# Side steps of a two-block layer kernel on one core: attention, gate and second output set apart, delta-rule scores on unscaled keys

## The chip, the cores and the metric

The kernel runs on one core of one Trainium2 chip. The metric is the time of one execution on the device in microseconds (us). The engines' names in the profile are PE (TensorE, matmuls and 128x128 transposes), PEld (its weight loads), DVE (VectorE), ACT (ScalarE), POOL (GpSimd) and SP (SyncE, here the queue that loads the weights).

## The reference, cut to what matters

256 tokens of width 2048, fp32 throughout. Two blocks follow each other. The first projects the normed input to an mLSTM and a gated delta rule, gates their outputs and projects them back. The second is attention over dilated windows beside a gated linear attention (GLA), then a feed-forward part of width 5632.

```python
# first block: the delta rule, 16 heads of 128, chunks of 64
qkv = _causal_conv_silu(dn_qkv, dn_conv_w)
dq = _l2norm(_heads(dq, DN_HEADS)); dk_ = _l2norm(_heads(dk_, DN_HEADS))
kk = jnp.einsum('cbhtd,cbhsd->cbhts', kc, kc)
a_mat = jnp.where(strict, bc[..., :, None] * kk * decay_mat, 0.0)
lhs = a_mat + jnp.eye(CHUNK, dtype=a_mat.dtype)
rhs = jnp.concatenate([vc * bc[..., None], kc * (bc * jnp.exp(gam))[..., None]], axis=-1)
sol = lax.linalg.triangular_solve(lhs, rhs, left_side=True, lower=True, unit_diagonal=True)
# second block: gate of the GLA, attention weights
log_a_f = jax.nn.log_sigmoid(lr_f @ gla_gate_w_fwd[l] + gla_gate_b_fwd[l]) / GLA_GATE_TAU
p = jnp.exp(logits - m); s = jnp.sum(p, axis=-1, keepdims=True)
gla_out = (_merge_heads_2(o).astype(x.dtype) * gla_norm_w[l]) * jax.nn.silu(gr)
mixed = jnp.concatenate([attn_out, gla_out], axis=-1) @ w_out[l]
```

The kernel solves the triangular system by inverting 32-wide diagonal blocks and joining them to blocks of 64 and 128 (the last level covers a whole tile of 128 tokens, so the chunk of 64 need not be kept).

## The kernel before, in words

All large products are fp32 products made of three reduced ones: weight_hi with x_hi, weight_lo with x_hi, weight_hi with x_lo. ACT makes weight_hi as a rounded copy of the raw weights, DVE makes weight_lo as the difference. The products are cut into 780 half slots (`HALVES`, `NH`). On PE a half slot is its side steps and then one product of 12 matmuls of 128x512 (`product`, lines L1323 to L1325). In a half slot s ACT and DVE do their side steps too, and `split(s + 3)`: ACT the weight_hi copy of 128x1024 (L1351), which waits for product s − 1, DVE the weight_lo difference (L1749). SP loads a chunk of 1 MB raw weights for two half slots at a time, five half slots or so ahead of use.

Everything else is a side step. `side_table()` puts each step's name at a half slot with `put(slot, step, ...)`, mostly counted from `END[job]`, the half slot behind a job's last product; each engine runs its part of the steps in the order of this one table, ahead of that slot's product or split. POOL and SP run theirs in the table's order alone. A step waits on semaphores for the parts of other engines that it needs (`at("dve:alog", half, c)`). Buffers of 128x1024 (blocks of the `arena`) and four side banks of PSUM are given out by `block_table` and `bank_table`, from the steps' lifetimes.

The steps that the change touches:

- Delta rule, four groups g of four heads. From s = `END[dz{g}]` + 1: `dk` (eight transposes of k on PE, squares with accumulation on ACT, a Square of q's 128x1024), `dss` (sums of q's squares by 16 matmuls with a column of ones, L961; then a power on POOL and the factors on DVE), `dkscale` (DVE scales k by the factor ck, which is the inverse norm times beta), `dkc` (eight transposes back, evicted to block kt), `drhs`, `ddecay`, `dmask` (decays and masks), `dsc` (scores of k with kt and of q), `nout`/`nin` (32-wide blocks to DRAM and back, one per partition), `dinv` (their inverses, some 65 operations on POOL, end L2335), `tout`/`tin` (back), `dT` (transposed), `dX`/`dY` for widths 64 and 128 (`LEVELS`; joins), `dv`, `du0`, `dbu`, `du1`, `do` (values, solution, output), `donorm`, `dgate`, `dout`.
- mLSTM, in the same stretch: `msq` (norm of the output; POOL's power of 128x4), `mgated` (DVE's four products), `mout` (PE's transposes).
- Gate of the GLA: `ggate2` (ACT: Abs, Exp, Ln of 128x1024 one behind the other, L1614 to L1616), `ggate3` (DVE).
- Attention: two halves, four pairs c of heads each. `alog` (PE's scores of 128x256, L1261; DVE adds the bias and takes the maximum, L2172; ACT's exponentials with sums, L1663), `anorm` (DVE reciprocal L2177, POOL multiply of 128x1024, L2279), `aturn` (eight transposes, L888), `apv`.
- Second output, in the second block: `ggated` (DVE's four products of 128x256, L1755), `gout` (eight transposes), twice, for hp 0 and 1.

L888, L1351, L1749, L1752, L1755 and L2279 are lines of helpers (transpose, copy, tensor_tensor, tensor_scalar, scalar_tensor_tensor, POOL's tensor_tensor).

## Time and profile before

| | |
|---|---|
| median of 3 runs | 2401.85 us (2401.59 to 2402.27) |
| the profiled execution, its own time | 2399.88 us |
| its span | 2398.2 us |
| granted clock of PE, mean | 0.997 |
| busy PE, DVE, ACT, POOL | 99%, 59%, 50%, 10% |
| product matmuls on PE (three lines, two kinds of input) | 9312 |
| weights from DRAM | 423.59 MB read, 179 GB/s over the span |

The own time of the profiled execution is its span and what lies around it. Matmul rows show length from a modelled end, so neighbours overlap; the distance between two starts is what one costs. A row with "x4" holds four instructions. The granted clock is in parts of full speed, 2.4 GHz; 0.50 is 1.2 GHz.

### The profile page before, as it was taken

What the parts mean: (1) busy time and instruction counts of PE and PEld (TensorE: products, weight loads), DVE (VectorE), ACT (ScalarE), POOL (GpSimd) and SP (SyncE); (2) the same over time, 40 slices, a digit from 0 to 9 for tenths busy, and PEclk for the clock granted to TensorE, in tenths of its full rate; (3) what the DMA queues carried; (4) which work ended last, traced back from release to release, by engine and by line L of the source; (5) the groups of instructions that cost most, each with busy time, mean ns of one, the idle gap of its engine ahead of it and who ended that gap; (6) DMA issues with size and microseconds to landing.
All of it is one profiled execution on the core that took longest, in us unless ns stands there. A gap on an engine that the chain in (4) does not pass through costs nothing.

```text
span 2398.2 us, 28559 instructions
## 1 busy us (share of the span) xinstructions
PE 2374.9 (99%) x11522; PEld 1948.8 (81%) x11522; DVE 1426.6 (59%) x1689; ACT 1189.5 (50%) x1653; POOL 233.3 (10%) x332
## 2 busy tenths in 40 slices
PE   9999999999999999999999999999999999999998
PEld 7888888888888888888887778678888888888886
DVE  6655665565566545665865555566554555556775
ACT  6544453454445345555646445466444444446664
POOL 0052004205200430000000010100000000000000
PEclk9999999999999999999999999999999999999999
DMA  6555455455545554765674444456655665555554
GB/s 209 194 171 163 143 191 171 149 172 171 163 141 192 170 165 161 237 202 196 213 232 157 151 157 139 141 176 221 194 186 188 193 193 185 189 188 193 193 194 140
DMA packets 235969, 430.72 MB, mean 180 GB/s; under 512 B 27492, under 2 KB 30445, under 8 KB 235838
## 3 DMA queue, kind: packets, MB, share of 16 engines
q1 hardware_dynamic: 222848, 413.30, 52.5%
q10 hardware_dynamic: 12990, 15.60, 2.2%
q8 instruction: 91, 1.49, 0.2%
q14 instruction: 40, 0.33, 0.0%
HBM read 423.59 MB, written 5.28 MB: 179 GB/s over the span
## 4 chain that ended last, share of the span: by engine, by line
PE 95%; DVE 2%; ACT 2%; issue 1%; POOL 0%; ACTq 0%; POOLq 0%; DVEq 0%
PE gemm L1323 29%; PE gemm L1325 28%; PE gemm L1324 28%; PE side L888 3%; DVE weight_lo L1749 1%; PE side L993 1%; PE side L1246 1%; ACT weight_hi L1351 1%; ACT arena L1663 0%; DVE arena L1749 0%; PE side L1285 0%; PE side L898 0%; DVE stats L2172 0%; PE side L1059 0%; PE side L997 0%
## 5 line engine op out<-in xcount | busy, mean ns | idle before, releaser
L1749 DVE TENSOR_TENSOR weight_lo<-weight_raw,weight_hi 128x1024 fp32r<-128x1024 f32 x780 | 971.0, 1248 | 775.6 <-ACT weight_hi L1351 775.2
L1351 ACT ACTIVATE weight_hi<-weight_raw 128x1024 fp32r<-128x1024 f32 x780 | 821.7, 1056 | 825.0 <-PE gemm L1325 806.8
L1323 PE MATMUL gemm<-weight_hi,x_hi 128*128 128x512 f32 x2368 | 943.8, 399 | 3.4 <-DVE x_lo L1755 2.1
L1325 PE MATMUL gemm<-weight_hi,x_lo 128*128 128x512 f32 x2368 | 924.3, 390 | 0.0
L1324 PE MATMUL gemm<-weight_lo,x_hi 128*128 128x512 f32 x2368 | 923.3, 390 | 0.0
L1323 PEld LDWEIGHTS gemm<-weight_hi,x_hi 128*128 128x128 f32 x2368 | 445.8, 188 | 103.2 <-issue 12.0
L1325 PEld LDWEIGHTS gemm<-weight_hi,x_lo 128*128 128x128 f32 x2368 | 445.2, 188 | 94.9
L1324 PEld LDWEIGHTS gemm<-weight_lo,x_hi 128*128 128x128 f32 x2368 | 446.0, 188 | 89.4 <-issue 1.4
L1323 PE MATMUL gemm<-weight_hi,lhs_hi 128*128 128x512 f32 x736 | 287.1, 390 | 0.0
L1325 PE MATMUL gemm<-weight_hi,lhs_lo 128*128 128x512 f32 x736 | 286.4, 389 | 0.0
L1324 PE MATMUL gemm<-weight_lo,lhs_hi 128*128 128x512 f32 x736 | 286.4, 389 | 0.0
L2279 POOL TENSOR_TENSOR stats<-stats,minus_half 128x4 f32<-128x4 f32 (+4 forms) x20 | 28.1, 1407 | 1886.8 <-DVE stats L1752 1886.6
L1325 PEld LDWEIGHTS gemm<-weight_hi,lhs_lo 128*128 128x128 f32 x736 | 138.2, 188 | 28.7
L1324 PEld LDWEIGHTS gemm<-weight_lo,lhs_hi 128*128 128x128 f32 x736 | 138.2, 188 | 28.5
L1323 PEld LDWEIGHTS gemm<-weight_hi,lhs_hi 128*128 128x128 f32 x736 | 138.2, 188 | 28.4
L1749 DVE TENSOR_TENSOR lhs_lo<-arena,lhs_hi 128x512 fp32r<-128x512 f32 x184 | 125.9, 684 | 0.5 <-ACT lhs_hi L1351 0.5
L2279 POOL TENSOR_TENSOR arena<-arena 128x60 f32<-128x60 f32 (+25 forms) x252 | 120.2, 477 | 33.0 <-DMA arena<-delta_blocks 13.6
L1351 ACT ACTIVATE arena<-side 128x512 f32<-128x512 f32 (+2 forms) x101 | 53.8, 570 | 132.3 <-PE side L888 57.7
L1351 ACT ACTIVATE lhs_hi<-arena 128x512 fp32r<-128x512 f32 x184 | 113.4, 616 | 1.1 <-PE gemm L1325 1.1
L888 PE MATMUL side<-constants,arena 128*128 128x128 f32 (+3 forms) x662 | 89.1, 276 | 9.4 <-POOL arena L2279 7.7
L888 PEld LDWEIGHTS side<-constants,arena 128*128 128x128 f32 (+3 forms) x662 | 77.1, 142 | 22.8 <-POOL arena L2279 9.3
L1420 ACT ACTIVATE arena<-gemm,stats 128x512 f32<-128x512 f32 x66 | 41.8, 686 | 44.7 <-PE gemm L1325 44.7
(189 smaller groups left out, 1035.6 us busy)
## 6 DMA issues: line engine op xcount, KB each, us to landing
weight_raw<-in_w_in_dram SPq DMA_DIRECT2D x207, 1024.0 KB, 5.1
weight_raw<-in_w_out_dram SPq DMA_DIRECT2D x48, 1024.0 KB, 5.0
weight_raw<-in_w_gate_dram SPq DMA_DIRECT2D x44, 1024.0 KB, 5.1
weight_raw<-in_w_up_dram SPq DMA_DIRECT2D x44, 1024.0 KB, 5.1
weight_raw<-in_w_down_dram SPq DMA_DIRECT2D x44, 1024.0 KB, 5.0
arena<-rel_line ACTq DMA_DIRECT2D x8, 384.0 KB, 5.3
arena<-in_x_dram SPq DMA_DIRECT2D x4, 512.0 KB, 9.7
arena<-delta_blocks ACTq DMA_DIRECT2D x16, 128.0 KB, 5.1
```

The source lines that it names most:

```text
L888: return e.transpose(o, i, IDN[0:n, 0:n])
L993: m = e.matmul(p[:, (h % 2) * T:(h % 2 + 1) * T], yk[:, h * T:h * T + P], y[:, h * T:(h + 1) * T], start=True, stop=True)
L1246: m = e.matmul(o, *both[x][z], start=z == 0, stop=z == len(both[x]) - 1)
L1323: e.matmul(pair[i][:, :], xh[:, s], wh, start=first, stop=False)
L1324: e.matmul(pair[i][:, :], xh[:, s], wl, start=False, stop=False)
L1325: m = e.matmul(pair[i][:, :], xl[:, s], wh, start=False, stop=last)
L1351: return e.activation(o, i, ACT.Copy, scale=scale)
L1420: s = e.activation(part(b, i), pair_of(key)[i][:, :], ACT.Tanh, scale=hr[:, i:i + 1])
L1749: return e.tensor_tensor(o, x, y, op)
L2279: return e.tensor_tensor(o, x, y, op)
```

## The change

The delta rule: q and k are each transposed seven half slots behind the end of their job (`dnorm`), ACT squares them in PSUM with accumulation, and the ones-matmuls, the scaled copy of k, its transposes and block kt are gone. The scores are between unscaled k. The factor ck is put on where results are evicted: for the 32-wide blocks it goes to DRAM (`cout`, 1024 elements of 4 bytes, written with a non-contiguous side) and back with one value per row (`nout`), and POOL multiplies the blocks of 128x1024 by it at the head of `dinv`; for `dX` the copy on ACT becomes a multiply on DVE; for `dbu` the subtraction becomes four operations that multiply by −ck and add. Everything from `dT` on comes one half slot later.

The gate: ACT's three functions become three steps (`ggabs`, `ggexp`, `ggln`), each direction's in other half slots, with Exp of both directions in one and Ln of both in one.

Attention: the exponentials become a step `aexp` two half slots behind `alog`; `anorm` is one half slot earlier and stands ahead of the next `alog`. Transposes stay.

Second output: `ggated` and `gout` of hp = 1 come one half slot later.

```diff
-        put(s, "dk", g, 0), put(s, "dk", g, 1)
-        put(s + 1, "dss", g)
-        put(s + 2, "dkscale", g)
-        put(s + 4, "dkc", g, 0), put(s + 4, "dkc", g, 1)
+        for key in (f"dk{g}", f"dq{g}"):
+            put(END[key] + 7, "dnorm", key, 0), put(END[key] + 7, "dnorm", key, 1)
+        put(s + 1, "dss", g), put(s + 3, "cout", g)
...
-        put(s + 30, "dT", g, 0), put(s + 30, "dT", g, 1)
+        put(s + 31, "dT", g, 0), put(s + 31, "dT", g, 1)
...
-        put(s + 46, "dout", g, 0), put(s + 46, "dout", g, 1)
+        put(s + 47, "dout", g, 0), put(s + 47, "dout", g, 1)
...
-        put(s + 4 + 4 * d, "ggate2", d), put(s + 7 + 4 * d, "ggate3", d)
+        put(s + 4 + d, "ggate2", d), put(s + 6 + d, "ggabs", d)
+        put(s + 8, "ggexp", d), put(s + 10, "ggln", d), put(s + 12 + d, "ggate3", d)
...
-            put(s + 4 + 2 * c, "alog", half, c), put(s + 7 + 2 * c, "anorm", half, c)
+            put(s + 4 + 2 * c, "alog", half, c), put(s + 6 + 2 * c, "aexp", half, c)
+            put(s + 6 + 2 * c, "anorm", half, c)
             put(s + 9 + 2 * c, "aturn", half, c)
...
-    put(t + 1, "ggated", hp), put(t + 2, "gout", hp, 0), put(t + 2, "gout", hp, 2)
+    put(t + 1 + hp, "ggated", hp), put(t + 2 + hp, "gout", hp, 0), put(t + 2 + hp, "gout", hp, 2)
...
+        def cout(g):
+            w.wait_ge(*at("dve:dss:ck", g))
+            e.dma_start(c_dram[g].rearrange("n p -> p n"), stat(NT * HB, "ck", g),
+                        allow_slow_non_contiguous=True).then_inc(sem("dma:cout"), 16)
...
+            src = bass.AP(tensor=c_dram.tensor, offset=g * NT * HB * P, ap=[[0, NSUB], [SUB, P // NSUB], [1, SUB]])
+            w.wait_ge(*at("dma:cout", g))
+            e.dma_start(blk("S", g)[:, 3 * SUB * SUB // 4:3 * SUB * SUB // 4 + SUB], src).then_inc(sem("dma:cin"), 16)
...
-        def dss(g):
-            w.wait_ge(*at("act:dk", g, 0))
-            p, sq = open_bank("dss", g), blk("sq", g)
-            for i in range(NT):
-                for h in range(HB):
-                    m = e.matmul(p[:, i * HB + h:i * HB + h + 1], sq[:, h * T + i * P:h * T + (i + 1) * P], ONE[:, 0:1],
-                                 start=True, stop=True)
-            m.then_inc(sem("pe:dss"))
...
-            y = blk("kt", g) if q in (0, 1, 4) else blk("y", f"dq{g}")
+            y = yk if q in (0, 1, 4) else blk("y", f"dq{g}")
...
-            if i == 0:
-                sq = claim("sq", g)
-                w.wait_ge(*at("dve:convsilu", f"dq{g}"))
-                e.activation(sq, blk("y", f"dq{g}"), ACT.Square)
...
+        def dnorm(key, i):
+            g, p = number_of(key), bank("dnorm", key, i)
+            z = i * HB + (NT * HB if kind_of(key) == "dk" else 0)
+            w.wait_ge(*at("pe:dnorm", key, i))
             for h in range(HB):
+                s = e.activation(p[:, h * P:(h + 1) * P], p[:, h * P:(h + 1) * P], ACT.Square,
+                                 accum_out=stat(4 * HB, "squares", g)[:, z + h:z + h + 1])
...
+        def dX(g, wd):
+            X, p, hw, ck = blk("X", g), bank("dX", g, wd), wd // 2, stat(NT * HB, "ck", g)
+            w.wait_ge(*at("pool:dinv:zero", g))
+            w.wait_ge(*at("dve:dss:ck", g))
+            w.wait_ge(*at("pe:dX", g, wd))
+            rows, cols = (slice(0, P), slice(0, T)) if wd < P else (slice(hw, P), slice(X6, BLK))
+            tt(X[rows, cols].rearrange("p (n x) -> p n x", x=hw), p[rows, 0:2 * HB * hw].rearrange("p (n x) -> p n x", x=hw),
+               over(ck[rows, :], 2, hw), ALU.mult).then_inc(sem("dve:dX"))
...
-            tt(b, b, bank("dbu", g), ALU.subtract).then_inc(sem("dve:dbu"))
+            w.wait_ge(*at("dve:dss:ck", g))
+            p, nck = bank("dbu", g), stat(NT * HB, "nck", g)
+            for h in range(HB):
+                sl = slice(h * P, (h + 1) * P)
+                s = stt(b[:, sl], p[:, sl], nck[:, HB + h:HB + h + 1], b[:, sl], ALU.mult, ALU.add)
...
             w.wait_ge(*at("dma:unit", g))
+            w.wait_ge(*at("dma:cin", g))
+            after(tt(N, N, over(blk("S", g)[:, 3 * SUB * SUB // 4:3 * SUB * SUB // 4 + SUB], 1, SUB), ALU.mult))
```

In the order of PE's instructions, before, at the half slot behind the gate sums (`fsum` is L932 to L935; gemm_0 and gemm_1 are the products' PSUM tiles):

```order
L1323 MATMUL gemm_1<-weight_hi,x_hi 128x512
L1324 MATMUL gemm_1<-weight_lo,x_hi 128x512
L1325 MATMUL gemm_1<-weight_hi,x_lo 128x512
L932 MATMUL side<-gate_work,constants 128x8
L933 MATMUL side<-gate_work,constants 128x8
L934 MATMUL side<-gate_work,constants 128x8
L935 MATMUL side<-gate_work,constants 128x8
L1323 MATMUL gemm_0<-weight_hi,x_hi 128x512
```

The same place on PE in the changed kernel, where L893 is the transpose:

```order
L1311 MATMUL gemm_1<-weight_hi,x_hi 128x512
L1312 MATMUL gemm_1<-weight_lo,x_hi 128x512
L1313 MATMUL gemm_1<-weight_hi,x_lo 128x512
L937 MATMUL side<-gate_work,constants 128x8
L938 MATMUL side<-gate_work,constants 128x8
L939 MATMUL side<-gate_work,constants 128x8
L940 MATMUL side<-gate_work,constants 128x8
L893 MATMUL side<-constants,arena 128x128 x8
L1311 MATMUL gemm_0<-weight_hi,x_hi 128x512
```

The eight transposes of the first group's k have come in directly behind the gate sums.

On DVE at the start of attention's first half, before (L2172 is the maximum in `alog`, L2177 the reciprocal in `anorm`):

```order
L1749 TENSOR_TENSOR arena<-side,arena 128x256 x4
L2172 TENSOR_REDUCE stats<-arena 128x4
L1752 TENSOR_SCALAR stats<-stats 128x4
L1749 TENSOR_TENSOR weight_lo<-weight_raw,weight_hi 128x1024 x2
L1749 TENSOR_TENSOR arena<-side,arena 128x256 x4
L2172 TENSOR_REDUCE stats<-arena 128x4
L1752 TENSOR_SCALAR stats<-stats 128x4
L1749 TENSOR_TENSOR weight_lo<-weight_raw,weight_hi 128x1024
L2177 RECIPROCAL stats<-stats 128x4
L1749 TENSOR_TENSOR weight_lo<-weight_raw,weight_hi 128x1024
```

The same place on DVE in the changed kernel, with L2157 the maximum and L2162 the reciprocal:

```order
L1726 TENSOR_TENSOR arena<-side,arena 128x256 x4
L2157 TENSOR_REDUCE stats<-arena 128x4
L1729 TENSOR_SCALAR stats<-stats 128x4
L1726 TENSOR_TENSOR weight_lo<-weight_raw,weight_hi 128x1024 x2
L2162 RECIPROCAL stats<-stats 128x4
L1726 TENSOR_TENSOR arena<-side,arena 128x256 x4
L2157 TENSOR_REDUCE stats<-arena 128x4
L1729 TENSOR_SCALAR stats<-stats 128x4
L1726 TENSOR_TENSOR weight_lo<-weight_raw,weight_hi 128x1024 x2
```

The reciprocal of the first pair now stands ahead of the second pair's bias and maximum, not behind them and a weight_lo.

On POOL at the head of an inverse, before (the two MEMSETs are the head of `dinv`, the line above them is the mask of `dmask`):

```order
L2279 TENSOR_TENSOR arena<-arena,stats 128x512
L2322 MEMSET arena 128x1024
L2323 MEMSET arena 128x1024
L2279 TENSOR_TENSOR arena<-arena 128x31 x2
L2279 TENSOR_TENSOR arena<-arena 128x30 x2
```

The same place on POOL in the changed kernel:

```order
L2264 TENSOR_TENSOR arena<-arena,stats 128x512
L2307 MEMSET arena 128x1024
L2308 MEMSET arena 128x1024
L2264 TENSOR_TENSOR arena<-arena 128x1024
L2264 TENSOR_TENSOR arena<-arena 128x31 x2
L2264 TENSOR_TENSOR arena<-arena 128x30 x2
```

A multiply of the whole block has come in ahead of the substitution; behind the inverse in the second and fourth group POOL's next instruction is the mLSTM's power of 128x4, before and after.

## Rows read from the trace of the kernel before

**Rows 1.** The page's busy time, share of the span and instructions of each engine

```profile
PE 2374.9 (99%) x11522; PEld 1948.8 (81%) x11522; DVE 1426.6 (59%) x1689; ACT 1189.5 (50%) x1653; POOL 233.3 (10%) x332
```

**Rows 2.** The waits: engine and line, releaser, total, times, longest

```profile
PE side L888 <- POOL arena L2279: 7.7, 3, 3.0
```

**Rows 3.** PE's timeline, 118 to 132 us: start, length, instruction, [idle before, releaser]

```profile
118.04 0.47 PE L1323 MATMUL gemm<-weight_hi,x_hi 128*128 128x512 f32 x1
...
122.59 0.49 PE L1323 MATMUL gemm<-weight_hi,x_hi 128*128 128x512 f32 x1
...
125.45 0.39 PE L1323 MATMUL gemm<-weight_hi,x_hi 128*128 128x512 f32 x1
...
128.17 0.39 PE L1323 MATMUL gemm<-weight_hi,x_hi 128*128 128x512 f32 x1
...
131.69 0.48 PE L1323 MATMUL gemm<-weight_hi,x_hi 128*128 128x512 f32 x1
```

**Rows 4.** The timeline at the first half's first transposes, 1401 to 1420 us

```profile
1401.90 0.39 PE L1323 MATMUL gemm<-weight_hi,x_hi 128*128 128x512 f32 x1
...
1404.48 0.51 ACT L1663 ACTIVATE arena<-arena,stats 128x256 f32<-128x256 f32 x1 [4.67 <-DVE stats L1752]
...
1405.78 0.50 PE L1323 MATMUL gemm<-weight_hi,x_hi 128*128 128x512 f32 x1
...
1408.94 2.79 POOL L2279 TENSOR_TENSOR arena<-arena,stats 128x1024 f32<-128x1024 f32 x1 [49.95 <-DVE stats L2177]
...
1419.38 0.49 PE L1323 MATMUL gemm<-weight_hi,x_hi 128*128 128x512 f32 x1
```

**Rows 5.** A window: busy us of each engine, then PE clock, DMA share, GB/s

```profile
1411.00:1416.00 5.00, 4.22 (x14) 3.74 (x15) 2.34 (x5) 2.14 (x9) 0.72 (x1) 0.50 0.70 245
```

**Rows 6.** PE's timeline in the second half of attention

```profile
1497.35 0.50 PE L1323 MATMUL gemm<-weight_hi,x_hi 128*128 128x512 f32 x1
...
1508.96 0.50 PE L1323 MATMUL gemm<-weight_hi,x_hi 128*128 128x512 f32 x1
...
1520.86 1.10 PE L888 MATMUL side<-constants,arena 128*128 128x128 f32 x8 [2.54 <-POOL arena L2279]
```

**Rows 7.** PE's timeline behind the gate functions

```profile
1281.34 0.50 PE L1323 MATMUL gemm<-weight_hi,x_hi 128*128 128x512 f32 x1 [1.29 <-DVE weight_lo L1749]
```

**Rows 8.** The timeline at the second output: DVE, PE, DVE

```profile
1572.90 1.67 DVE L1755 SCALAR_TENSOR_TENSOR arena<-arena,stats 128x256 f32<-128x256 f32 x4
...
1574.62 1.09 PE L888 MATMUL side<-constants,arena 128*128 128x128 f32 x8 [1.71 <-DVE arena L1755]
...
1575.62 0.69 DVE L1749 TENSOR_TENSOR lhs_lo<-arena,lhs_hi 128x512 fp32r<-128x512 f32 x1
```

**Rows 9.** The timeline behind the gate sums: DVE, PE

```profile
59.06 1.22 DVE L1755 SCALAR_TENSOR_TENSOR arena<-arena 128x1024 f32<-128x1024 f32 x1
...
59.70 0.49 PE L1323 MATMUL gemm<-weight_hi,x_hi 128*128 128x512 f32 x1
```

**Rows 10.** The timeline behind the second group's inverse: POOL, DVE, PE

```profile
439.05 1.01 POOL L2279 TENSOR_TENSOR stats<-stats,minus_half 128x4 f32<-128x4 f32 x1
...
441.51 1.65 DVE L1755 SCALAR_TENSOR_TENSOR arena<-side,stats,arena 128x256 f32<-128x256 f32 x4
...
444.44 1.04 PE L888 MATMUL side<-constants,arena 128*128 128x128 f32 x8
```

**Rows 11.** POOL's timeline at the next multiply of attention

```profile
1418.30 1.90 POOL L2279 TENSOR_TENSOR arena<-arena,stats 128x1024 f32<-128x1024 f32 x1 [6.58 <-DVE stats L2177]
```

**Rows 12.** The timeline at the first group's subtraction: DVE, PE

```profile
250.58 0.69 DVE L1749 TENSOR_TENSOR arena<-arena,side 128x512 f32<-128x512 f32 x1 [0.82 <-PE side L1071]
...
253.05 1.05 PE L1059 MATMUL side<-arena 128*128 128x128 f32 x8
```

**Rows 13.** DMA issues from 202 to 212 us: count, KB each, us to landing

```profile
weight_raw<-in_w_in_dram SPq DMA_DIRECT2D x2, 1024.0 KB, 5.2
...
delta_inverses<-arena SPq DMA_DIRECT2D x4, 32.0 KB, 3.9
```

More of the change, by code:

```diff
@@ L376 @@
     "conv": ("convturn", "convtap", "convsilu"),
-    "delta": ("dk", "dss", "dkscale", "dkc", "drhs", "ddecay", "dmask", "dsc", "dinv", "dT", "dX", "dY", "dv", "du0",
+    "delta": ("dnorm", "dss", "drhs", "ddecay", "dmask", "dsc", "dinv", "dT", "dX", "dY", "dv", "du0",
               "dbu", "du1", "do", "donorm", "dgate", "dout"),
@@ L523, in bank_table @@
     t = []
[L524 to L525 removed]
+    same = {"cols0": "dve", "cols": "dve", "fsum": "dve", "rel1": "dve", "dnorm": "act", "dsc": "dve",
+            "dT": "act", "dX": "dve", "dv": "dve", "du0": "act", "dbu": "dve", "du1": "act", "do": "dve", "dout": "act",
             "chan": "act", "mdec": "dve", "mturn": "act", "mout": "act", "gscore": "dve",
@@ L535, in bank_table @@
             t.append((step, step, (("dve:convtap",) + args,), None))
-        elif name == "dk":
-            t.append((step, step, (("dve:dkscale", args[0]),), None))
         elif name == "ddecay":
@@ L851, in tout @@
                 e.dma_start(to[q], S[q * SUB:(q + 1) * SUB]).then_inc(sem("dma:tout"), 16)
-        steps = dict(nout=nout, tout=tout)
+        steps = dict(cout=cout, nout=nout, tout=tout)
         x_load(0)
@@ L947, in convturn @@
             turn_pair(p, blk("raw", key), c).then_inc(sem("pe:convturn"))
[L949 to L951 removed]
+        def dnorm(key, i):
+            w.wait_ge(*at("dve:convsilu", key))
+            p, y = open_bank("dnorm", key, i), blk("y", key)
             for h in range(HB):
                 m = turn(p[:, h * P:(h + 1) * P], y[:, h * T + i * P:h * T + (i + 1) * P])
[L954 to L970 removed]
+            m.then_inc(sem("pe:dnorm"))
         def ddecay(g):
@@ L1609, in gload, with ggabs, ggexp, ggln @@
                 load(part(gbias, d), a[f"gla_gate_b_{s}_2"].broadcast_to([P, NC]), "dma:gload")
-        def ggate2(d):
-            la, lt = blk("la", d), claim("lt", d)
+        def ggabs(d):
+            lt = claim("lt", d)
             w.wait_ge(*at("dve:ggate2", d))
-            w.wait_ge(w.own, w.mark(e.activation(lt, la, ACT.Abs)))
-            w.wait_ge(w.own, w.mark(e.activation(lt, lt, ACT.Exp, scale=-1.0)))
-            e.activation(lt, lt, ACT.Ln, bias=1.0).then_inc(sem("act:ggate2"))
+            e.activation(lt, blk("la", d), ACT.Abs).then_inc(sem("act:ggabs"))
+        def ggexp(d):
+            w.wait_ge(*at("act:ggabs", d))
+            e.activation(blk("lt", d), blk("lt", d), ACT.Exp, scale=-1.0).then_inc(sem("act:ggexp"))
+        def ggln(d):
+            w.wait_ge(*at("act:ggexp", d))
+            e.activation(blk("lt", d), blk("lt", d), ACT.Ln, bias=1.0).then_inc(sem("act:ggln"))
         def gsum(hp, d):
@@ L1654, in gout, with aexp @@
             s.then_inc(sem("act:gout"))
-        def alog(half, c):
+        def aexp(half, c):
             E, nm, sums = blk("E", half, c), stat(2 * NT, "nm", half, c), stat(2 * NT, "sums", half, c)
@@ L1907, in dss @@
             after(ts(rk, r[:, 1], 0.5, ALU.mult))
-            tt(ck, rk, beta, ALU.mult).then_inc(sem("dve:dss:ck"))
-        def dkscale(g):
-            kc, ck = blk("kc", g), stat(NT * HB, "ck", g)
-            w.wait_ge(*at("dve:dss:ck", g))
-            for i in range(NT):
-                s = tt(heads(kc, i), by_head(bank("dk", g, i)), over(ck[:, i * HB:(i + 1) * HB], 2, P), ALU.mult)
-            s.then_inc(sem("dve:dkscale"))
+            after(tt(ck, rk, beta, ALU.mult))
+            ts(nck, ck, -1.0, ALU.mult).then_inc(sem("dve:dss:ck"))
         def ddecay(g):
@@ L2175, in anorm @@
         def anorm(half, c):
-            w.wait_ge(*at("act:alog", half, c))
+            w.wait_ge(*at("act:aexp", half, c))
             e.reciprocal(stat(2 * NT, "ainv", half, c), stat(2 * NT, "sums", half, c)).then_inc(sem("dve:anorm"))
```

92 lines of the change are left out of this document (31 added, 61 removed).

## The prediction

> **What bounds the kernel now.** I read the page's list of engines first: TensorE (PE) is busy 99% of the span, VectorE (DVE) 59%, ScalarE (ACT) 50%, GpSimd (POOL) 10% [rows 1]. So the time is the sum of what PE does plus the few places where it stands. The reader is to see two consequences: an instruction taken off DVE, ACT or POOL gains nothing by itself, and only three things can change the time: PE instructions added or removed, a wait of PE added or removed, and the clock that PE gets.
>
> The waits come second. What PE waits for among the side work is short: transposes that wait for POOL, 7.7 us in three waits, the longest 3.0 [rows 2]. The rest lies in single rows below. Third is the timeline of PE, from the start of one product (12 matmuls of 128x512) to the next. A half slot with no side work takes 128.17 − 125.45 = 2.72 us; one with eight 128x128 transposes 131.69 − 128.17 = 3.52; one with the 128x1 matmuls of the norms 122.59 − 118.04 = 4.55, and the product behind it still 122.59 to 125.45 = 2.86, 0.14 over [rows 3]. One with an attention score step takes 1405.78 − 1401.90 = 3.88 [rows 4]. These are the prices of everything PE does here.
>
> **The change part by part.**
>
> *Delta rule, PE.* In each of four groups the second set of eight transposes (of the scaled k) goes and eight transposes of q come in: 16 before, 16 after, at 0.80 for eight, so zero. The ones-matmuls go: 4.55 − 2.72 + 0.14 = 1.97 us a group [rows 3], four times: **−7.9**. This is the surest term, as it is PE time with nothing beside it.
>
> *Attention.* Before, ACT's exponentials stand in the half slot of the scores, and ACT stands 4.67 us for DVE there [rows 4]; behind them on ACT wait the next weight_hi copies, behind those DVE's weight_lo, and the reciprocal comes behind the next score step's place in PE's order. POOL's multiply so starts at 1408.94 and ends at 1411.73, 3.0 us after PE wants to transpose its result [rows 2, 4]. Behind this wait PE's granted clock is 0.50 (1.2 of 2.4 GHz) in the stretch 1411 to 1416 [rows 5]. So the wait costs more than its own length: from 1405.78 to 1419.38 are 13.60 us for two half slots, one with transposes (3.52) and one with scores (3.88), 6.2 us over. In the second half the same pair takes 1508.96 − 1497.35 = 11.61, 4.2 over, and a later transpose waits 2.54 [rows 6]. After, exponentials come two half slots behind the scores, the reciprocal is ahead of the next scores on DVE, and the transposes keep their place, five half slots behind the scores. From exponentials to transposes are then three half slots, at least 8.2 us, for four exponentials (4 x 0.5), a reciprocal of four columns and POOL's 2.79 [rows 4]: about 5, so some 3 us to spare. ACT no longer stands for DVE. All three waits go, and with them the slow stretch: **−13.0** (6.2 + 4.2 + 2.54). What is late next is nothing on PE: the weight_lo halves are made three half slots ahead.
>
> *Gate.* Three functions a direction stood together on ACT, ahead of its weight_hi copies; PE had to wait 1.29 for a weight_lo [rows 7]. Spread over slots 4 to 10, none is longer than two functions: **−1.3**.
>
> *Second output.* PE waits 1.71 for DVE's four products, which start at 1572.90 and take 1.67 [rows 8]. Moved one half slot on, PE comes 2.72 later: 1572.91 + 2.72 = 1575.63. But DVE now does the pair weight_lo and lhs_lo first, 1576.31 − 1574.57 = 1.74, so its four products end at 1572.90 + 1.74 + 1.67 = 1576.31, and PE waits 0.7 still: **−1.0**, ends 0 (DVE gets a further eviction in front) and −1.7.
>
> *Transposes of k and q placed by their job's end.* The first stands at once behind the gate sums. DVE makes its input at 59.06 to 60.28; PE would begin 59.70 [rows 9]: **+0.6**, ends 0 and 1.2 (DVE one weight_lo later).
>
> *The factor.* It reaches the 32-wide blocks by POOL's multiply of 128x1024 at the head of the inverse; the same size takes POOL 2.79 and 1.90 elsewhere [rows 4, 11]. No row shows it with a stride here; 1.90 to 2.79 are my bounds. The inverse so ends that much later. Queued behind it on POOL in groups 1 and 3 is the power for the mLSTM norm (439.05); on that hangs DVE's product that ends 441.51 + 1.65 = 443.16, and PE's transposes at 444.44 [rows 10]. The slack is 1.28, so PE waits 0.6 to 1.5, twice: 1.2 to 3.0, I take **+2.1**. In groups 0 and 2 the power does not stand there; the inverse itself has some slots in hand till the DMA that takes it away. I count nothing, and for the upper end the same 0.6 to 1.5 there too (6.0 in all).
>
> The Trainium skill has a rule that speaks against this edit ("SBUF — State Buffer", section "Who interferes with whom"): a DVE operation with two SBUF inputs and a GpSimd operation that reads SBUF hold a shared port in turn, whoever issues first, so the multiply may also hold DVE's weight_lo. The two lengths of the same POOL multiply, 2.79 and 1.90, agree with it [rows 4, 11]. By it a weight_lo would come up to 1.9 late four times; being made three half slots ahead, it changes the sum by nothing.
>
> *Evictions.* The wide blocks' copies go from ACT to DVE as a multiply, and the last subtraction becomes four operations of 128x128. Before, that subtraction starts 250.58 and PE needs it at 253.05 [rows 12]; four products of twice the width take 1.65 [rows 10], which ends 252.23, so 0.8 is left: zero. The multiplies of 128x256 are below the 0.69 of a 128x512 [rows 12], with a half slot (2.72) until PE needs them: zero; upper end 0.5. The delta rule's end one half slot on keeps the steps' distances; its waits move along: zero.
>
> *DMAs.* Eight small ones more. The factor's way out stands in SP's queue ahead of weights, and is 1024 elements of 4 bytes. Four writes of the inverses, 32 KB each in rows of 32 elements (128 bytes, so 256 pieces), landed in 3.9 us median beside weights that took 5.2 [rows 13]. A weight lands five half slots before its use: 5 x 2.72 − 5.2 = 8.4 us in hand. Zero.
>
> Here too the Trainium skill speaks against it ("DMA: Bandwidth & Descriptors", section "Rules for kernel authors"): a non-contiguous last dimension is taken apart into one descriptor per element. The trace's small pieces, above, were not slow enough to matter; none as small as 4 bytes is in it. What it would give is the slower rival below.
>
> **Sum.** −7.9 − 13.0 − 1.3 − 1.0 + 0.6 + 2.1 = **−20.5 us**. The profiled execution took 2399.88 (span 2398.2), so 2379.4 for such an execution; it was 1.97 below the median of 2401.85, which I carry over: **2381.3 us**. The ends: −7.9 − 13.0 − 1.3 − 1.7 = −23.9 (2378.0), and −7.9 − 13.0 − 1.3 + 0 + 1.2 + 6.0 + 0.5 = −14.5 (2387.4).
>
> **Rivals.**
> 1. *POOL's multiply is hidden*: the inverse waits for its input's DMA anyway and something in its chain gives. For it: only 1.28 of slack is lacking. Against: the order on POOL is fixed. −22.6, about 2379. Chance 0.2.
> 2. *Attention keeps one wait a half*: ACT or DVE is still behind at the first transposes. For it: the first of each half is the costliest now. Against: the 3 us to spare above. Then 6.2 + 4.2 stay: 2381.3 + 10.4 = 2391.7. Chance 0.13.
> 3. *Slower: the factor's DMA blocks the weights.* Place: SP's queue at the third half slot behind the norms, four times. If small pieces are worked off one after another, 1024 take four times the 3.9 of 256, 15.6 us, which is 7.2 over the 8.4 in hand; at 4 x 7.2 = 29 the time is 2410. For the time to be above before's, the DMA must hold the queue for 8.4 + 20.5/4 = 13.5 us. Against: those four DMAs, 1024 pieces together, passed side by side without a wait of ACT or PE. Chance 0.04.
> 4. *Little happens*: PE's waits are moved and not removed (new ones at the delta rule's DVE hand-overs eat some 17 us). No row speaks for so much. About 2398. Chance 0.03.
>
> **How the numbers follow.** The forecast has 0.6, and its own range is 2378.0 to 2387.4. With rival 1, which lies inside, this is 0.8. I widen it a little, to 2377 to 2388.5, as the sum has terms of tenths that I set to zero; rivals 2 to 4 are left out. This kernel's measurement tells 0.2% (4.8 us) from no change. Faster by more than that: forecast, rivals 1 and 2, 0.93. Within: rival 4 and a bit of 2 and 3, 0.03. Slower: 0.04.
>
> **What would show it.** No 128x1 matmuls in PE's list, and half slots in the delta rule of 2.72 or 3.52 only. The transposes waiting for POOL in attention gone from the waits, and granted clock near 1.00 all through there. No wait before the product after the gate functions. A wait of about 0.7 at the second output's transposes, 0.6 behind the gate sums, and about 1 each at the mLSTM output's transposes in groups 1 and 3, not in 0 and 2. The prediction is wrong if ACT waits for weight DMAs behind the factor's DMA, if PE waits at the blocks that DVE now evicts, or if a slow clock appears elsewhere, since that costs several us for a wait of 2 to 3.

## The result, and the profile after

The changed kernel takes 2382.48 us (median of 4 runs, 2381.47 to 2383.26) against 2401.72 (4 runs, 2399.98 to 2402.27): a ratio of 0.9921, 95% interval 0.9904 to 0.9938. The forecast was 2381.3, faster. The two profiled executions took 2382.65 and 2399.88, 17.2 us apart; the terms below are read from those two. The other 2 us of the medians' distance are not in the trace: the profiled execution of before was below all four timed ones, and single executions of one kernel differ by 2.

The page of the changed kernel, first part, answers to [rows 1]:

```profile
PE 2364.4 (99%) x11458; PEld 1938.3 (81%) x11458; DVE 1425.4 (60%) x1701; ACT 1184.1 (50%) x1695; POOL 241.6 (10%) x336
```

PE has 10.5 us less work, in instructions that went and in a clock that no longer falls; the rest are waits. In the waits of the changed kernel the entry of [rows 2] is gone and a smaller one of PE has come (third line). ACT now waits for weights five times, where it waited once before, and DVE waits longer for the inverse:

```profile
ACT weight_hi L1339 <- DMA weight_raw<-in_w_in_dram: 14.5, 5, 4.7
...
DVE arena L1726 <- POOL arena L2322: 8.4, 2, 4.2
...
PE side L893 <- DVE arena L1732: 2.7, 5, 0.8
```

The first two entries before:

```profile
ACT weight_hi L1351 <- DMA weight_raw<-in_w_in_dram: 4.8, 1, 4.8
...
DVE arena L1749 <- POOL arena L2335: 2.5, 2, 1.4
```

I compared the start of each half slot's product in the two traces. The distance between neighbouring starts changes at more than seventy places; most of these only move a step (eight transposes leave one half slot and come into another). The table has what is left when such moves are set off against each other:

| part | forecast, us | in the traces, us |
|---|---|---|
| ones-matmuls gone, 4 groups | −7.9 | −7.9 |
| attention | −13.0 | −12.7 |
| gate functions | −1.3 | −1.9 |
| second output | −1.0 | −1.2 |
| first k's transposes behind the gate sums | +0.6 | +0.7 |
| mLSTM output transposes, groups 1 and 3 | +2.1 | +0.4 and +1.0 |
| groups 0 and 2, products that wait | 0 | +0.7, +0.7 and +0.8 |
| third group's q, transposes | 0 | +1.0 |
| smaller ones in the delta rule, under 0.2 each | 0 | +0.6 |
| start of the first product | 0 | +0.7 |
| sum | −20.5 | −17.2 |

The last row but one is the time until the first product starts, 12.0 before and 12.7 after, ahead of everything changed; in the kernels below it is anywhere from 12.0 to 13.5. The rows of the delta rule vary too. The kernel u_delta below has its delta rule as before; against it the five places of the new waits behind the inverses (rows six and seven) hold 3.4 us in this trace, but 2.0 to 2.2 in u_attn, u_gate and exp_only, whose delta rule is this one.

*Attention.* PE and POOL at the first half's first transposes, changed kernel; the lines answer to [rows 4]: POOL's multiply, the product behind a score step, the transposes, the product behind the next score step:

```profile
1395.41 1.90 POOL L2264 TENSOR_TENSOR arena<-arena,stats 128x1024 f32<-128x1024 f32 x1 [39.77 <-DVE stats L2162]
...
1402.43 0.50 PE L1311 MATMUL gemm<-weight_hi,x_hi 128*128 128x512 f32 x1
...
1405.29 1.03 PE L893 MATMUL side<-constants,arena 128*128 128x128 f32 x8
...
1410.05 0.50 PE L1311 MATMUL gemm<-weight_hi,x_hi 128*128 128x512 f32 x1
```

POOL is done at 1397.31, eight microseconds ahead of the transposes. The two half slots take 1410.05 − 1402.43 = 7.62, where [rows 4] had 13.60 and my base was 7.40. A window of the changed kernel that lies in them answers to [rows 5], with the clock third from the end:

```profile
1402.00:1407.00 5.00, 5.00 (x30) 3.99 (x27) 3.00 (x8) 3.72 (x12) 1.90 (x1) 1.00 0.72 263
```

The clock is 1.00 and not 0.50. (What the slow clock was worth is another question; u_attn below answers it.) POOL's multiply is 1.90 in all eight cases now. Before, the first of each half took 2.79, beside a weight_lo of DVE; that agrees with the Trainium skill ("SBUF — State Buffer", "Who interferes with whom"), as read ahead of the result.

*Second output and gate sums*, changed kernel, answers to [rows 8] and [rows 9]: DVE's products and the transposes that wait for them, in each case:

```profile
59.80 1.22 DVE L1732 SCALAR_TENSOR_TENSOR arena<-arena 128x1024 f32<-128x1024 f32 x1
...
61.08 1.09 PE L893 MATMUL side<-constants,arena 128*128 128x128 f32 x8 [0.48 <-DVE arena L1732]
...
1558.36 1.67 DVE L1732 SCALAR_TENSOR_TENSOR arena<-arena,stats 128x256 f32<-128x256 f32 x4
...
1560.08 1.09 PE L893 MATMUL side<-constants,arena 128*128 128x128 f32 x8 [0.53 <-DVE arena L1732]
```

Both waits are there, 0.48 and 0.53 where 0.6 and 0.7 were forecast.

*Behind the inverses*, changed kernel. First groups 1 and 3, which answer to [rows 10]: the end of the inverse (L2322), the power, DVE's products, the transposes:

```profile
438.48 0.66 POOL L2322 COPY arena<-arena 128x256 f32<-128x256 f32 x1
439.00 1.00 POOL L2264 TENSOR_TENSOR stats<-stats,minus_half 128x4 f32<-128x4 f32 x1
...
441.45 1.65 DVE L1732 SCALAR_TENSOR_TENSOR arena<-side,stats,arena 128x256 f32<-128x256 f32 x4
...
443.15 1.09 PE L893 MATMUL side<-constants,arena 128*128 128x128 f32 x8 [0.19 <-DVE arena L1732]
...
863.72 1.09 PE L893 MATMUL side<-constants,arena 128*128 128x128 f32 x8 [0.75 <-DVE arena L1732]
```

Against [rows 10] POOL is no later in microseconds from the start (439.00 against 439.05): its multiply began at 401.76, 2.2 before the inverse's first operation of the kernel before (403.92). But PE arrives 1.5 us earlier, mostly since the ones-matmuls ahead have gone, so the slack went from the other end. Then group 0, where a step of the mLSTM's decays (`mdec`) on DVE waits for the inverse, the transposes of the third group's q, and group 2:

```profile
201.10 0.69 DVE L1726 TENSOR_TENSOR arena<-side,gate_work 128x512 f32<-128x512 f32 x1 [4.17 <-POOL arena L2322]
...
204.35 0.50 PE L1311 MATMUL gemm<-weight_hi,x_hi 128*128 128x512 f32 x1 [0.36 <-DVE weight_lo L1726]
...
509.58 1.09 PE L893 MATMUL side<-constants,arena 128*128 128x128 f32 x8 [0.78 <-DVE arena L1732]
...
632.58 1.28 ACT L1521 ACTIVATE arena<-arena,stats 128x128 f32<-128x128 f32 x4 [4.10 <-issue]
...
636.12 0.50 PE L1311 MATMUL gemm<-weight_hi,x_hi 128*128 128x512 f32 x1 [0.47 <-DVE weight_lo L1726]
```

DVE's 4.17 (1.06 at this place before) puts its weight_lo behind, and PE waits. At 632.58 ACT has stood 4.10 (2.95 before) at the issue of `tin`, which waits for the inverse's way out; its weight_hi is late, then DVE's weight_lo, then PE.

*POOL's multiply*, changed kernel, in the first group, and the weight_lo of DVE beside it:

```profile
166.90 2.41 POOL L2264 TENSOR_TENSOR arena<-arena 128x1024 f32<-128x1024 f32 x1 [3.68 <-DMA arena<-delta_blocks]
```

```profile
168.17 2.22 DVE L1726 TENSOR_TENSOR weight_lo<-weight_raw,weight_hi 128x1024 fp32r<-128x1024 f32 x1 [2.07 <-ACT weight_hi L1339]
```

It takes 2.41, in the middle of the bounds (2.39 to 2.41 in all four groups). DVE's weight_lo, which starts behind it, takes 2.22 and not 1.2. This agrees with the Trainium skill's rule ("SBUF — State Buffer", "Who interferes with whom") that was weighed ahead of the result; PE has no wait there.

*The factor's DMA*, changed kernel, DMA issues from 130 to 150 us, then those from 132 to 134 us alone, and one of ACT's waits for weights in the fourth group; the first row answers to [rows 13]:

```profile
weight_raw<-in_w_in_dram SPq DMA_DIRECT2D x4, 1024.0 KB, 10.7
delta_factors<-stats SPq DMA_DIRECT2D x1, 4.0 KB, 14.5
```

```profile
weight_raw<-in_w_in_dram SPq DMA_DIRECT2D x1, 1024.0 KB, 14.5
```

```profile
802.70 1.06 ACT L1339 ACTIVATE weight_hi<-weight_raw 128x1024 fp32r<-128x1024 f32 x1 [3.27 <-DMA weight_raw<-in_w_in_dram]
```

The 4 KB take 14.5 us (13.0 to 14.6 in the four groups). The 10.7 is the median of four loads; the two issued directly behind the factor take 14.5 and 13.7, in place of 5. In between the core's transfers all but stop; here are three stretches, with GB/s at the end of the line.

```profile
131.00:136.00 5.00, 5.00 (x24) 4.13 (x23) 3.39 (x4) 2.12 (x2) 0.00 (x0) 1.00 1.16 277
136.00:143.00 7.00, 7.00 (x28) 4.66 (x27) 2.21 (x4) 3.66 (x8) 2.48 (x2) 1.00 1.06 24
143.00:148.00 5.00, 5.00 (x24) 4.15 (x23) 3.44 (x3) 2.12 (x3) 5.00 (x4) 1.00 0.88 297
```

ACT waits for these weights 1.3 to 3.3 us once a group; PE never does.

### The profile page after: what moved, and what is told of

It is laid out like the page before. It is cut to its first block, busy times and chain, and to the rows that moved or that the text cites. A ratio compares the mean times of both kernels' runs of the same rounds, so it can differ in the third digit from the quotient of the medians.

```text
span 2380.8 us, 28492 instructions
## 1 busy us (share of the span) xinstructions
PE 2364.4 (99%) x11458; PEld 1938.3 (81%) x11458; DVE 1425.4 (60%) x1701; ACT 1184.1 (50%) x1695; POOL 241.6 (10%) x336
## 2 busy tenths in 40 slices
DMA packets 240658, 430.81 MB, mean 181 GB/s; under 512 B 32180, under 2 KB 35133, under 8 KB 240526
## 4 chain that ended last, share of the span: by engine, by line
PE 89%; POOL 5%; DVE 2%; DMA 1%; issue 1%; ACT 1%; ACTq 0%; SPq 0%; POOLq 0%; DVEq 0%
PE gemm L1311 27%; PE gemm L1313 27%; PE gemm L1312 27%; POOL arena L2264 5%; PE side L893 3%; DMA arena<-delta_blocks 1%; DVE arena L1732 1%; DVE weight_lo L1726 1%; PE side L1234 1%; PE side L981 0%; PE side L903 0%; PE side L1249 0%; PE side L1273 0%; ACT weight_hi L1339 0%; PE side L1047 0%
## 5 line engine op out<-in xcount | busy, mean ns | idle before, releaser
L2264 POOL TENSOR_TENSOR arena<-arena 128x28 f32<-128x28 f32 (+26 forms) x256 | 128.6, 502 | 34.1 <-DMA arena<-delta_blocks 14.3
L1339 ACT ACTIVATE arena<-side 128x512 f32<-128x512 f32 (+1 forms) x85 | 45.8, 577 | 124.5 <-PE side L893 78.1
L893 PE MATMUL side<-constants,arena 128*128 128x128 f32 (+3 forms) x662 | 87.3, 273 | 2.7 <-DVE arena L1732 2.7
L893 PEld LDWEIGHTS side<-constants,arena 128*128 128x128 f32 (+3 forms) x662 | 76.1, 140 | 16.1 <-DVE arena L1732 4.5
```

Source lines behind the costliest of these rows:

```text
L893: return e.transpose(o, i, IDN[0:n, 0:n])
L1339: return e.activation(o, i, ACT.Copy, scale=scale)
L2264: return e.tensor_tensor(o, x, y, op)
```

## The experiments

**One part undone at a time.** From the changed kernel, attention, gate and second output each put back; and the kernel before with those three put in, which is the changed kernel without its delta part.

```diff
# u_attn
-            put(... s + 6 + 2 * c, "aexp", half, c)
-            put(s + 6 + 2 * c, "anorm", half, c)
+            put(... s + 4 + 2 * c, "aexp", half, c)
+            put(s + 7 + 2 * c, "anorm", half, c)
# u_gate
-        put(s + 4 + d, "ggate2", d), put(s + 6 + d, "ggabs", d)
-        put(s + 8, "ggexp", d), put(s + 10, "ggln", d), put(s + 12 + d, "ggate3", d)
+        put(s + 4 + 4 * d, "ggate2", d), put(s + 4 + 4 * d, "ggabs", d)
+        put(s + 4 + 4 * d, "ggexp", d), put(s + 4 + 4 * d, "ggln", d), put(s + 7 + 4 * d, "ggate3", d)
# u_gout
-    put(t + 1 + hp, "ggated", hp), put(t + 2 + hp, "gout", hp, 0), put(t + 2 + hp, "gout", hp, 2)
+    put(t + 1, "ggated", hp), put(t + 2, "gout", hp, 0), put(t + 2, "gout", hp, 2)
```

> The changed kernel with attention's part undone: exponentials again in the half slot of the scores, reciprocal and multiply again behind the next scores. Theory (three waits of TensorE at attention's transposes, two of them with a slow clock behind): it gives back 12.7 us of the 2382.5, so about 2395.2, with PE's waits for POOL at 7 to 8 us in three waits and a clock near 0.5 behind the first. Rival (the waits were due to the delta rule's or the gate's part shifting PE): no more than 3 us, about 2385.

Measured: 2396.13 us (10 runs, 2393.3 to 2397.7), 13.7 above the changed kernel. PE's rows with a wait there, which answer to [rows 2, 6] (the second line is a transpose step that the kernel before had no wait at):

```profile
1407.78 1.09 PE L893 MATMUL side<-constants,arena 128*128 128x128 f32 x8 [2.99 <-POOL arena L2264]
...
1418.67 0.66 PE L893 MATMUL side<-constants,arena 128*128 128x128 f32 x4 [1.44 <-DVE arena L1726]
...
1426.52 1.10 PE L893 MATMUL side<-constants,arena 128*128 128x128 f32 x8 [0.69 <-POOL arena L2264]
...
1498.17 1.97 PE L893 MATMUL side<-constants,arena 128*128 128x128 f32 x8 [2.17 <-POOL arena L2264]
...
1516.50 1.09 PE L893 MATMUL side<-constants,arena 128*128 128x128 f32 x8 [2.54 <-POOL arena L2264]
```

And its windows behind the first and the fourth of these, clock third from the end:

```profile
1407.00:1412.00 5.00, 4.22 (x24) 3.43 (x26) 2.35 (x5) 2.14 (x9) 0.72 (x1) 1.00 0.68 251
1498.00:1503.00 5.00, 4.83 (x18) 4.22 (x19) 1.84 (x5) 3.16 (x10) 0.12 (x1) 0.66 0.33 127
```

The fourth is in the second half. The waits are back and the time with them; the theory holds. But the clock that I expected near 0.5 behind the first wait was 1.00 in this execution, though the wait was as long as before (2.99 and 2.98): whether a wait of 2 to 3 us brings the clock down is not settled by its length alone. The spread of this kernel's runs goes with it: the two slowest have a mean clock of 0.996, the fastest 0.998.

The trace also tells what the slow clock was worth in the first half. Counted by starts against the changed kernel, that half is 5.7 us longer here at full clock and was 6.0 longer in the kernel before at half clock. With the fast clock PE only came sooner to the next results that were late: the new wait of 1.44, and 0.69 at the last. So in these two traces nearly all of the 6 us is ACT, DVE and POOL being late, and the slow stretch hid in it. The spread of the runs says that it is not free in every execution.

> The changed kernel with the gate's part undone: Abs, Exp and Ln of a direction again in one half slot. Theory: a wait of 1.3 to 1.5 us before a product behind the second Ln comes back and the first direction's placing costs 0.4 more, 1.9 in all, about 2384.4. Rival (the wait was hidden by attention's stall later and its removal was worth nothing): 2382.5.

Measured: 2382.91 us (4 runs), 0.4 above. End to end the rival looks better. In the trace it is not: PE's product waits 1.27 for weight_lo at 1278.18 again, and from `ggate2` to there the starts are 1.75 further apart (1.9 with the product behind), as in the table. The execution's first product started 0.5 earlier, and the waits in groups 0, 2 and 3 happened to be 1.2 shorter.

> The changed kernel with the second output's part undone (both steps of hp 1 one half slot earlier again). Theory: TensorE's wait for the four products grows from 0.53 to 1.7, plus 1.2 us, about 2383.7. Rival (DVE is earlier here now, since attention no longer holds it up): the wait is no longer there and the time is 2382 or less.

Measured: 2382.98 us (4 runs), 0.5 above. The transposes wait 1.71 again where it was 0.53, and the starts there are 1.18 further apart. The theory holds in the trace; terms of 1 to 2 us can't be told end to end.

> The kernel before with the parts for attention, gate and second output put in, and the delta rule as before. Theory: the delta part is worth little net, 7.9 us of ones-matmuls less some 5.8 of new waits, 2.1 in all, so this kernel is near 2384.6. Rival (the new waits are noise or taken from elsewhere, the delta part is worth its 7.9): 2390.

Measured: 2385.27 us (4 runs, 2384.66 to 2385.78), 2.8 above the changed kernel; 2.2 in the traces, from the third product to the end of the delta rule (ahead of that, this execution has a stretch of slow clock at its start, which the changed kernel's has not). The delta rule's part is worth about a third of the 7.9 that it takes off PE.

**Which half of the attention edit.**

```diff
# exp_only
             put(... s + 6 + 2 * c, "aexp", half, c)
-            put(s + 6 + 2 * c, "anorm", half, c)
+            put(s + 7 + 2 * c, "anorm", half, c)
# norm_only
-            put(... s + 6 + 2 * c, "aexp", half, c)
+            put(... s + 4 + 2 * c, "aexp", half, c)
             put(s + 6 + 2 * c, "anorm", half, c)
```

> Attention with the exponentials two half slots behind the scores, but reciprocal and multiply behind the next scores as before. Theory of the prediction (ACT's stand for DVE at the exponentials is the cause): all three waits gone, within 1 us of 2382.5. Rival (the place of the reciprocal behind the next pair's scores on DVE is the cause): waits of 2 to 3 us remain, 2390 or more.

> Attention with the reciprocal ahead of the next scores, but the exponentials in the half slot of the scores as before. Theory of the prediction (exponentials are the cause): waits of 2 us and more remain, 2390 or more. Rival (the reciprocal's place is the cause): all three gone, within 1 us of 2382.5.

Measured: exponentials moved alone 2382.20 us (4 runs), no wait of PE in attention. Reciprocal moved alone 2388.96 (4 runs, 2388.3 to 2390.5), 6.5 above. PE's waits with the reciprocal alone, two in the first half of attention, one in the second, and the window behind this last one:

```profile
1414.31 1.08 PE L1273 MATMUL side<-arena 128*64 128x256 f32 x8 [1.55 <-ACT arena L1339]
...
1417.91 0.66 PE L893 MATMUL side<-constants,arena 128*128 128x128 f32 x4 [1.93 <-DVE arena L1726]
...
1511.80 0.50 PE L1311 MATMUL gemm<-weight_hi,x_hi 128*128 128x512 f32 x1 [1.87 <-DVE weight_lo L1726]
```

```profile
1512.00:1517.00 5.00, 5.00 (x16) 3.90 (x16) 4.14 (x4) 3.79 (x6) 2.79 (x1) 0.66 0.79 245
```

ACT's stand for DVE ahead of the exponentials is gone with the first edit and is still 4.7 us with the second. So the prediction's cause is the right one: ACT standing for DVE in the half slot of the scores. The reciprocal's place alone takes half away and moves the rest onto other steps behind ACT and DVE; once the exponentials are moved, it is worth nothing.

**POOL's multiply.**

```diff
# no_mult (and the squared inverse norm in dmask)
-            after(tt(N, N, over(blk("S", g)[:, 3 * SUB * SUB // 4:3 * SUB * SUB // 4 + SUB], 1, SUB), ALU.mult))
# mult_x2: the line twice
```

> The changed kernel without POOL's multiply at the head of the inverse (the decay masks take the squared inverse norm instead so that the numbers keep their size; the factor beta is left out of the 32-wide blocks). The factor's two DMAs stay. Theory: the new waits of TensorE in the delta rule come from POOL being late: 0.2 and 0.75 at the mLSTM's transposes of groups 1 and 3, 0.4 to 0.7 in groups 0 and 2 at products whose weight_lo is late, 0.7 in group 2. All go, about 3.5 us, so 2379.0. Rival (they come from the factor's way over DRAM): no change, 2382.5.

Measured: 2378.92 us (4 runs, 2378.7 to 2379.9), 3.6 faster. In its trace the starts come closer together at five places: 0.66 in group 0, 0.4 in group 1, 0.7 and 0.8 in group 2, 1.0 in group 3. These places are now as in u_delta, so the waits behind the inverses were due to the multiply, and the DMAs of the factor, which stayed, had no part. That the size came out to 0.1 us is in part luck: the changed kernel's trace, from which it was forecast, has these waits at 3.4, where three others have them at 2.0 to 2.2.

> The changed kernel with that multiply done twice (the factor is then squared in those blocks). Theory: each of the waits at the mLSTM's transposes and at the products in groups 0 and 2 grows by the length of one multiply, some 2 us: 4 x 2 = 8, and more if the clock falls behind one, about 2391. Rival (slack elsewhere in the chain takes it up): below 2384.5.

Measured: 2397.18 us (10 runs, 2396.3 to 2397.9), 14.7 slower: the direction is right, the size nearly twice that of the theory. POOL's pair and one of PE's waits, and three windows behind such waits, clock third from the end:

```profile
167.23 5.75 POOL L2264 TENSOR_TENSOR arena<-arena 128x1024 f32<-128x1024 f32 x2 [3.18 <-DMA arena<-delta_blocks]
```

```profile
875.43 1.97 PE L893 MATMUL side<-constants,arena 128*128 128x128 f32 x8 [3.09 <-DVE arena L1732]
```

```profile
447.00:452.00 5.00, 3.86 (x15) 3.44 (x16) 2.07 (x4) 2.08 (x5) 0.00 (x0) 0.66 0.83 242
632.00:637.00 5.00, 4.88 (x14) 3.89 (x15) 2.90 (x7) 3.22 (x7) 0.00 (x0) 0.66 0.80 235
875.00:880.00 5.00, 4.57 (x15) 3.99 (x16) 1.60 (x2) 2.79 (x6) 0.00 (x0) 0.50 0.79 238
```

The two take 5.75 together. If the first takes 2.4 as in the changed kernel, the second takes 3.3; a weight_lo of DVE overlaps both. The second multiply finds no slack: it lengthens the waits to 2.3 to 3.1, and behind three of the four the clock of the window is 0.50 or 0.66. The starts are 2.0, 3.7, 3.6 (less 0.7) and 5.1 further apart in the four groups: 13.7, plus 0.8 at the start.

**The factor's DMA.**

```diff
# cout_x3
-            e.dma_start(c_dram[g].rearrange("n p -> p n"), stat(NT * HB, "ck", g),
-                        allow_slow_non_contiguous=True).then_inc(sem("dma:cout"), 16)
+            for r in range(3):
+                e.dma_start(c_dram[g + 4 * r].rearrange("n p -> p n"), stat(NT * HB, "ck", g),
+                            allow_slow_non_contiguous=True).then_inc(sem("dma:cout"), 16)
# cout_flat
+            to = bass.AP(tensor=c_dram.tensor, offset=g * NT * HB * P, ap=[[NT * HB, P], [1, NT * HB]])
+            e.dma_start(to, stat(NT * HB, "ck", g)).then_inc(sem("dma:cout"), 16)
```

> The changed kernel with the factor's DMA of 1024 four-byte elements issued three times one behind the other (to separate places), at the same half slot. One takes 14.3 us and ACT waits 1.3 to 3.3 us for the weights behind it, PE not at all. Theory (the elements stand ahead of the weights, which have some 5 us left): two more are 28.6 later, 23 past the slack, four times, so near 2475, with PE waiting for weight_hi or weight_lo. Rival (weights run beside them and are only slowed): ACT's waits grow, PE's do not, 2382.5 to 2385.

> The changed kernel with the factor written to DRAM in rows of 32 bytes, 128 pieces in place of 1024 (the values then stand in another order, so the 32-wide blocks get factors of other rows; sizes and work are the same). Theory (the DMA reaches nothing that TensorE waits for): ACT's waits for weight DMAs in the delta rule go, the time stays within 0.5 us of 2382.5. Rival (its traffic makes SP, nout or nin late): 1 to 3 us faster, as POOL's inverse starts earlier.

Measured: three times 2434.06 us (4 runs, 2429.8 to 2435.8), 51.6 slower; flat 2382.31 (4 runs). With three, DMA issues, then ACT's and PE's wait in the second group:

```profile
delta_factors<-stats SPq DMA_DIRECT2D x12, 4.0 KB, 22.2
```

```profile
409.60 2.00 ACT L1340 ACTIVATE weight_hi<-weight_raw 128x1024 fp32r<-128x1024 f32 x2 [18.59 <-DMA weight_raw<-in_w_in_dram]
```

```profile
411.97 0.80 PE L1312 MATMUL gemm<-weight_hi,x_hi 128*128 128x512 f32 x1 [8.16 <-DVE weight_lo L1727]
```

Flat, its DMA issues from 130 to 150 us:

```profile
weight_raw<-in_w_in_dram SPq DMA_DIRECT2D x4, 1024.0 KB, 4.8
delta_factors<-stats SPq DMA_DIRECT2D x1, 4.0 KB, 4.7
```

The same 4 KB as 128 pieces of 32 bytes land in 4.7, and weights are at 4.8 again. ACT's waits in the delta rule are gone, but the time is the same to 0.2 us: the harm of one such DMA ends on ACT. With three the slower rival of the prediction happens: the starts are 7.4, 10.7, 10.8 and 9.5 further apart there (the clock behind is 0.50 in the window 162 to 167), 38 in all, and 14 more come behind the late inverses. The theory had the way right (PE waits for weight_lo) and the size nearly twice too large; the rival, that PE has no wait, is out. Three such DMAs don't take three times as long: the last of them lands 24 to 28 us behind its issue, where 43 were reckoned, and ACT's wait went from between 1.3 and 3.3 to between 15 and 19.

**A version with the new waits placed elsewhere.**

```diff
# best
-            put(END[key] + 7, "dnorm", key, 0), put(END[key] + 7, "dnorm", key, 1)
+            put(END[key] + 7 + (key in ("dk0", "dq2")), "dnorm", key, 0), ... (the same for 1)
-            put(s + 6, "mdec", G, n)
+            put(s + 7, "mdec", G, n)
-        put(s + 3, "mout", pr, 0), put(s + 3, "mout", pr, 2)
+        put(s + 3 + pr % 2, "mout", pr, 0), put(s + 3 + pr % 2, "mout", pr, 2)
-        put(s + 24, "tout", g), put(s + 27, "tin", g)
+        put(s + 24, "tout", g), put(s + 28, "tin", g)
-    put(t + 1 + hp, "ggated", hp), put(t + 2 + hp, "gout", hp, 0), ...
+    put(t + 1 + hp, "ggated", hp), put(t + 2 + 2 * hp, "gout", hp, 0), ...
# best2: of these, mdec
+            put(s + 6 + n // 2, "mdec", G, n)
```

> The changed kernel with the waits that it brought given another place in the table: transposes of the first k and of the third group's q one half slot on, the mLSTM's output transposes of odd groups, mdec and tin one half slot on, and the second output's transposes one more. Theory: each wait has more than a microsecond of slack by this, so they go: 0.67 + 1.0 + 1.35 + 1.3 + 0.8 + 0.64 = 5.8, so 2376.7. Rival (the steps moved meet others in their new half slots and wait there): 2380 or more.

Measured: 2377.91 us (4 runs, 2377.5 to 2378.2), a ratio to before of 0.9902 (0.9887 to 0.9917), 4.6 under the changed kernel. The first part of its page:

```profile
PE 2363.0 (99%) x11458; PEld 1938.1 (82%) x11458; DVE 1423.3 (60%) x1701; ACT 1184.9 (50%) x1695; POOL 244.2 (10%) x336
```

No row of PE behind 20 us has a wait for another engine. But in groups 0 and 2 the starts are 0.25, 0.28 and 0.13 over 2.72 in three half slots, as much as the wait that went: all three `mdec` steps on DVE now stand behind the inverse. The two traces are 5.1 apart, and 0.7 of it is a first product that starts earlier, so the new places are worth 4.4, where 5.8 were forecast.

> The kernel 'best' with only the third of DVE's three mdec steps one half slot on (the first two back in their place). In 'best' all three stand behind POOL's inverse, DVE waits 5.4 us and PE still waits 0.25, 0.28 and 0.13 in groups 0 and 2, as much as in the changed kernel. Theory (DVE's three evictions in a row behind the wait make weight_lo late): with two of them done ahead, the waits of these two groups go, 1.3 us less, about 2376.6. Rival (the wait for the inverse itself is what is late): no change, 2377.9.

Measured: 2377.70 us (4 runs, 2376.3 to 2378.4). Against the other the trace has 0.6 less at each of the two places, as the theory says, and a first product that starts 1.4 later; that is 1.2 in all, near the 1.3 forecast, but the medians differ by 0.2 and can't tell the two apart. With the late start set aside, its trace is the shortest of these kernels.

## Why the prediction was right

- **What bounds the kernel.** Right: the difference lies in PE's instructions, waits and clock. Taking 10 us of waits off ACT (cout_flat) moved nothing.
- **Ones-matmuls, −7.9.** Right to 0.1, as priced from [rows 3]. (They are eight in the program; the trace has 16 records of them a group, and PE's count fell by 64.)
- **Attention, −13.0.** Right, 12.7; the cause was the one named, as the two halves of the edit show. POOL now ends 8 us ahead of the transposes, where I had reckoned 3. What I said of the slow clock ("the wait costs more than its own length", and the slow stretch is the reason) is not borne out by the two traces: in u_attn the first half costs 5.7 at full clock, where it cost 6.0 at half clock. The number stayed right since it was read from starts.
- **Gate, −1.3; second output, −1.0.** 1.9 and 1.2. The gate's other 0.5 came from the first step's placing and from the product behind the wait, which I had not taken from the starts but from the wait alone.
- **POOL's multiply.** Its length (2.4) lies in the bounds. The mechanism in groups 1 and 3 was right, the size +1.4 for +2.1. I gave the slack as fixed, and in fact PE came earlier by what the change had saved ahead of that place, while the inverse began earlier too (2.2 and 1.9 us). That the sum of these moves came near my figure is luck in part.
- **"In groups 0 and 2 ... I count nothing"**: this step failed. It was worth 2.1 us, within the upper end that I kept for it, but by a way that I had not named: not the mLSTM's power, but an `mdec` step of DVE and the `tin` of ACT that wait for the inverse, with the weight halves queued behind them. In u_gate and exp_only the same places cost 1.1 to 1.2.
- **"seven half slots behind the end of the job ... zero"** for all but the first group: the third group's q waits 0.8 for DVE, which has six convolution steps, a weight_lo and two 128x1024 products in a row. I looked only at the first.
- **The factor's DMA.** Zero on PE was right; the reason, four DMAs of 128-byte rows in 3.9 us [rows 13], was wrong. It took 14.5, near the 15.6 of my slower rival and more than the 13.5 that I gave as the point from which the kernel is slower than before; and it was not slower. The weights behind it were up to 9.6 us late, a little over the 8.4 in hand, and ACT waited up to 3.3. I had named this wait as a sign that the prediction is wrong; it came, and cost nothing, as ACT and DVE make the weight halves three half slots ahead of PE. Only three such DMAs, with ACT's waits of 15 to 19, reached PE. The length itself agrees with the Trainium skill ("DMA: Bandwidth & Descriptors", "Rules for kernel authors"), whose rule on one descriptor per element I had weighed too low: 1024 pieces take 14.5, 128 pieces with the same bytes 4.7, and the page of the profile counts 32180 packets under 512 bytes with the first and 28596 with the second, 896 fewer for each of the four DMAs.
- **Sum.** −20.5 forecast, −17.2 in the two traces; the terms missed are 2.1 + 1.0 + 0.6 of small waits, and 0.7 at the start. The median moved by 19.2. So the terms are 3.3 off in the traces and the time is 1.2 off; the 2.0 between them is the spread of executions (the profiled one of before was below all timed ones), which no trace explains. That the time came out nearer than the terms is luck.

## What to carry to other kernels

Where one engine is at 99%, price an edit by the distance between starts on that engine, and for every step made later list each waiting instruction on the other engines with what is queued behind it. A wait of 4 us on DVE or ACT that nobody on the path needs still reaches PE through the weight halves behind it. A change that saves time ahead of a hand-over also takes slack from it. Test terms under 2 us in the trace, part by part, since end to end they vanish in how an execution starts, and compare more than one trace, since waits of some tenths differ between executions.

## What the runs showed of the hardware

- PE's clock after a wait, as the mean granted clock of a window of 5 us behind it: 0.50 behind 2.98 us and 0.66 behind 2.17 in the kernel before, 0.50 to 0.66 in three places of mult_x2 (2.3 to 3.1), and 0.66 behind 1.87 in norm_only. It was 1.00 behind 2.99 in u_attn, behind 2.36 in mult_x2 and behind 2.54 in the kernel before (window 1521 to 1526). So the length of the wait alone does not decide. In these traces no wait under 1 us was followed by a slow stretch.
- A DMA of 4 KB in 1024 four-byte elements took 14.5 us, and the two 1 MB weight loads behind it 14.5 and 13.7 in place of 5, with 24 GB/s moved over 7 us in between; as 128 pieces of 32 bytes it took 4.7. Three of the first kind one behind the other took 22.2 each (median), and ACT stood 15 to 19 us for weights.
- POOL's multiply of 128x1024 took 1.90 in attention, 2.79 there with a weight_lo of DVE that had started first, 2.40 at the head of the inverse (why it is not 1.90 there no run tells), and 3.3 as the second of two; a weight_lo of DVE that started behind one took 2.22 in place of 1.2.
